# The inverse of the delta rule's triangular matrices: whole 128x128 blocks, or diagonal 64x64 squares in 256 columns

## What is computed

```python
diff = G[..., :, None] - G[..., None, :]
decay = jnp.where(incl, jnp.exp(jnp.where(incl, diff, 0.0)), 0.0)
kk = jnp.einsum("bhnid,bhnjd->bhnij", kc, kc)
lower = jnp.where(strict, bc[..., :, None] * kk * decay, 0.0)
rhs = jnp.concatenate([vc * bc[..., None], kc * (bc * jnp.exp(G))[..., None]], axis=-1)
sol = lax.linalg.triangular_solve(lower + jnp.eye(CHUNK, dtype=f32), rhs, left_side=True,
                                  lower=True, unit_diagonal=True)
```

## Time and profile before

| | |
|---|---|
| median of 3 runs | 2357.48 us (2355.19 to 2358.24) |
| the profiled execution, its own time | 2354.87 us |
| its span | 2352.8 us, 30345 instructions |
| TensorE (PE) | 2188.8 us busy (93%) |
| weight loads (PEld) | 1770.9 us (75%) |
| VectorE (DVE) | 1203.7 us (51%) |
| ScalarE (ACT) | 964.8 us (41%) |
| GpSimd (POOL) | 777.5 us (33%) |
| chain that ended last | PE 74%, DVE 13%, issue 7%, ACT 4% |
| granted TensorE clock | 0.963 of full, mean |

### The profile page before, as it was taken

How to read it: one execution, slowest core, us unless ns; L and a number is a source line. 1 busy time by engine, 2 the same in 40 slices (tenths; PEclk the granted TensorE clock), 3 DMA queues, 4 the chain that set the end, 5 groups by cost and what they waited for, 6 DMA issues and landing times.

```text
span 2352.8 us, 30345 instructions
## 1 busy us (share of the span) xinstructions
PE 2188.8 (93%) x10326; PEld 1770.9 (75%) x10326; DVE 1203.7 (51%) x1824; ACT 964.8 (41%) x1605; POOL 777.5 (33%) x336
## 2 busy tenths in 40 slices
PE   3989898998899999989979999999999989999997
PEld 2768787786678888858847888888866667888886
DVE  6476968754333332269974333323666664333322
ACT  4343453533432332265544444322455554443321
POOL 2631313311344444400004444444311104444442
PEclk8999999999999999989989999999999899999999
DMA  3310201102223233211102233322100002233322
GB/s 120 108 54 28 63 28 46 39 25 77 76 86 94 96 105 99 91 45 54 45 27 84 95 98 98 125 98 82 64 19 18 18 10 90 97 98 98 106 98 72
DMA packets 43638, 169.01 MB, mean 72 GB/s; under 512 B 4848, under 2 KB 4912, under 8 KB 43056
## 3 DMA queue, kind: packets, MB, share of 16 engines
q1 hardware_dynamic: 43056, 163.82, 21.7%
q10 hardware_dynamic: 512, 4.24, 0.5%
HBM read 165.95 MB, written 2.10 MB: 71 GB/s over the span
## 4 chain that ended last, share of the span: by engine, by line
PE 74%; DVE 13%; issue 7%; ACT 4%; POOL 1%; DMA 1%; DVEq 0%; ACTq 0%; POOLq 0%; SPq 0%
PE bank L281 20%; PE bank L282 20%; PE bank L283 20%; PE bank L777 2%; PE bank L764 2%; ACT Pr L1974 1%; POOL WL L246 1%; DVE act_q L954 1%; DVE act_v L954 1%; PE bank L1916 1%; PE bank L1419 1%; PE bank L1418 1%; PE bank L1417 1%; DVE Pr L2092 1%; PE bank L768 1%
## 5 line engine op out<-in xcount | busy, mean ns | idle before, releaser
L246 POOL TENSOR_TENSOR WL<-raw,WR 128x1024 fp32r<-128x1024 f32 (+2 forms) x274 | 712.1, 2599 | 1049.0 <-ACT WR L242 1044.3
L281 PE MATMUL bank<-XR,WR 128*128 128x512 f32 x1528 | 619.6, 405 | 30.1 <-DVE XL L426 15.0
L282 PE MATMUL bank<-XL,WR 128*128 128x512 f32 x1528 | 599.7, 392 | 0.0
L283 PE MATMUL bank<-XR,WL 128*128 128x512 f32 x1528 | 599.2, 392 | 0.0
L242 ACT ACTIVATE WR<-raw 128x1024 fp32r<-128x1024 f32 (+2 forms) x230 | 256.2, 1114 | 758.5 <-PE bank L283 750.7
L281 PEld LDWEIGHTS bank<-XR,WR 128*128 128x128 f32 x1528 | 289.8, 190 | 105.9 <-issue 30.4
L281 PE MATMUL bank<-MR,WR 128*128 128x512 f32 (+1 forms) x856 | 339.3, 396 | 16.2 <-DVE ML L1586 7.6
L282 PEld LDWEIGHTS bank<-XL,WR 128*128 128x128 f32 x1528 | 290.2, 190 | 65.7 <-issue 8.3
L283 PEld LDWEIGHTS bank<-XR,WL 128*128 128x128 f32 x1528 | 289.8, 190 | 61.7
L282 PE MATMUL bank<-ML,WR 128*128 128x512 f32 (+1 forms) x856 | 336.2, 393 | 0.0
L283 PE MATMUL bank<-MR,WL 128*128 128x512 f32 (+1 forms) x856 | 336.0, 392 | 0.0
(11 more groups left out here) (304 smaller groups left out, 2667.5 us busy)
## 6 DMA issues: line engine op xcount, KB each, us to landing
raw<-w SPq DMA_DIRECT2D x224, 512.0 KB, 3.5
raw<-w SPq DMA_DIRECT2D x48, 704.0 KB, 4.0
raw<-w SPq DMA_DIRECT2D x16, 384.0 KB, 3.0
hT<-xT SPq DMA_DIRECT2D x1, 2048.0 KB, 7.5
hT<-xT ACTq DMA_DIRECT2D x1, 2048.0 KB, 7.7
out<-Y SPq DMA_DIRECT2D x8, 256.0 KB, 2.0
memT<-memT ACTq DMA_DIRECT2D x1, 1024.0 KB, 8.1
phi<-phi ACTq DMA_DIRECT2D x1, 1024.0 KB, 6.3
```

The lines of the kernel that those rows point to most:

```text
L246: nc.gpsimd.tensor_tensor(WL[:, here], raw[:, here], WR[:, here].bitcast(F32), ALU.subtract).then_inc(weight_split, 1)
L281: nc.tensor.matmul(into, wr, xr(k0 + k), start=start, stop=False)
L282: nc.tensor.matmul(into, wr, xl(k0 + k), start=False, stop=False)
L283: mm = nc.tensor.matmul(into, wl, xr(k0 + k), start=False, stop=stop)
```

## The change

Until the last level only the two diagonal 64x64 squares of each 128x128 block differ from zero. The change keeps them one above the other: an early square (rows 0 to 63) on partitions 0 to 63, a late one on 64 to 127, four chunks in 256 columns (`NARROW`). T and U of a head now share the tile "T" (`T_`, `U_`); "U" is written only at the end, its lower left part cleared once at the start.

- `square_products`: for each chunk and half one product of 64x64, operands and result on the same half of the partitions, both halves into one bank. `turn_squares`: the early square by a transpose, the late one by a product with the identity.
- kk: three products of 64 columns per chunk (early-early, late-late, late-early), the last kept as the corner.
- The masks are 64 wide; VectorE's and ScalarE's operations in levels 0 to 3 work on 128x256 instead of 128x512; L995 becomes two (early 64x256, late 64x512).
- Level 4's subtraction writes the squares to their places in "U" by two operations per head. Level 5 computes the corner alone: products of 64x64 on one quarter each, and VectorE writes the negative of the result (`tensor_scalar`). The corner is multiplied by beta at level 3's end in place of a mask product.
- The table of constants is 448 columns shorter. `HALF` in a later mixer is renamed `HALVES`.

The core of the diff:

```diff
+        def square_products(into, left, right):
+
+            for b in range(NB):
+                for half in HALVES:
+                    mm = nc.tensor.matmul(into[half, narrow(b)], left[half, narrow(b)], right[half, narrow(b)], start=True, stop=True)
+            return mm
+
+        def turn_squares(e, squares):
+            for b in range(NB):
+                nc.tensor.transpose(bank[6 + e][EARLY, narrow(b)], squares[EARLY, narrow(b)], ident[EARLY, EARLY])
+                mm = nc.tensor.matmul(bank[6 + e][LATE, narrow(b)], squares[LATE, narrow(b)], ident[LATE, LATE], start=True, stop=True)
+            return mm
...
-                    kb = G("keys", e)[:, of_chunk(b)]
-                    mm = nc.tensor.matmul(bank[6 + e][:, of_chunk(b)], kb, kb, start=True, stop=True)
+                    k_early, k_late = (G("keys", e)[:, of_half(b, h)] for h in BOTH)
+                    nc.tensor.matmul(bank[6 + e][EARLY, narrow(b, NARROW)], k_early, k_early, start=True, stop=True)
+                    nc.tensor.matmul(bank[6 + e][LATE, narrow(b, NARROW)], k_late, k_late, start=True, stop=True)
+                    mm = nc.tensor.matmul(bank[6 + e][LATE, narrow(b)], k_late, k_early, start=True, stop=True)
...
+                    if lv < LAST:
+                        square_products(bank[2 + e], joins, U_(e)).then_inc(s_["A_done"], 1)
+                        if lv:
+                            turn_squares(e, U_(e)).then_inc(s_["T_done"], 1)
+                    else:
                         for b in range(NB):
-                            mm = nc.tensor.transpose(bank[6 + e][:, of_chunk(b)], G("U", e)[:, of_chunk(b)], ident)
+                            mm = nc.tensor.matmul(bank[2 + e][EARLY, narrow(b)], G("lower", e)[LATE, narrow(b)], G("U", e)[LATE, of_half(b, 1)], start=True, stop=True)
+                        mm.then_inc(s_["A_done"], 1)
+                        for b in range(NB):
+                            mm = nc.tensor.transpose(bank[6 + e][EARLY, narrow(b)], G("U", e)[EARLY, of_half(b, 0)], ident[EARLY, EARLY])
                         mm.then_inc(s_["T_done"], 1)
...
-                    nc.scalar.activation(As[e], bank[2 + e][:, :], ACT.Identity).then_inc(s_["A_ready"], 1)
+                    nc.scalar.activation(As[e][rows, 0:NARROW], bank[2 + e][rows, 0:NARROW], ACT.Identity).then_inc(s_["A_ready"], 1)
...
-                    V.tensor_copy(G("T", 1), bank[7][:, :]).then_inc(s_["T_moved"][1], 1)
+                    V.tensor_copy(T_(1)[rows], bank[7][rows, 0:NARROW]).then_inc(s_["T_moved"][1], 1)
                 for e in BOTH:
                     dve.wait_ge(s_["U_done"], nth2(e, 6 * p + lv + 1))
-                    V.tensor_tensor(G("U", e), G("U", e), bank[4 + e][:, :], ALU.subtract).then_inc(s_["U_moved"], 1)
...
+                    if lv < LAST - 1:
+                        V.tensor_tensor(U_(e), U_(e), bank[4 + e][:, 0:NARROW], ALU.subtract).then_inc(s_["U_moved"], 1)
+                    elif lv == LAST - 1:
+                        for half in HALVES:
+                            ins = V.tensor_tensor(by_chunk(G("U", e))[half, :, half], by_chunk(U_(e)[half]), by_chunk(bank[4 + e][half, 0:NARROW]), ALU.subtract)
+                        ins.then_inc(s_["U_moved"], 1)
+                    else:
+                        V.tensor_scalar(by_chunk(G("U", e))[EARLY, :, LATE], by_chunk(bank[4 + e][EARLY, 0:NARROW]), -1.0, None, ALU.mult).then_inc(s_["U_moved"], 1)
```

More of the change, by code:

```diff
@@ L100 @@
 N_PARAMS = _at
-IDENT, ONES, TRI, LEVEL0 = 0, 1, 2, 3
-N_CONST = LEVEL0 + LEVELS
+IDENT, ONES, TRI = 0, 1, 2
+N_CONST = 3
+HALF = P // 2
+N_HALF = LEVELS
+HALF_IDENT = LEVELS - 1
 def constant_tables():
@@ L112, in constant_tables @@
     square[:, TRI] = p <= f
-    for s in range(LEVELS):
-        square[:, LEVEL0 + s] = (p >> (s + 1) == f >> (s + 1)) & (p >> s & 1 == 1) & (f >> s & 1 == 0)
+    half = np.zeros((P, N_HALF, HALF), np.float32)
+    r, c = p % HALF, np.arange(HALF)[None, :]
+    for s in range(LEVELS - 1):
+        half[:, s] = (r >> (s + 1) == c >> (s + 1)) & (r >> s & 1 == 1) & (c >> s & 1 == 0)
+    half[:, HALF_IDENT] = r == c
     dist = SEQ - P + p - np.arange(SEQ)[None, :]
@@ L662, in of_chunk, with of_half, narrow, by_chunk @@
             return slice(b * P, (b + 1) * P)
+        LAST = LEVELS - 2
+        HALVES = [slice(0, HALF), slice(HALF, P)]
+        EARLY, LATE = HALVES
+        NARROW = NB * HALF
+        def of_half(b, h):
+            return slice(b * P + h * HALF, b * P + (h + 1) * HALF)
+        def narrow(b, at0=0):
+            return slice(at0 + b * HALF, at0 + (b + 1) * HALF)
+        def by_chunk(tile):
+            return tile.rearrange("p (b n) -> p b n", b=NB)
+        def narrow_of(name, e):
+            return G(name, e)[:, 0:NARROW]
+        def T_(e):
+            return G("T", e)[:, 0:NARROW]
+        def U_(e):
+            return G("T", e)[:, NARROW:2 * NARROW]
         def conv_unit(p, kind, e):
@@ L737, in pair_tensor_g @@
                 pe.wait_ge(s_["T_ready"], nth2(e, c))
-                for b in range(NB):
-                    mm = nc.tensor.transpose(bank[6 + e][:, of_chunk(b)], G("T", e)[:, of_chunk(b)], ident)
-                mm.then_inc(s_["T_turned"], 1)
+                turn_squares(e, T_(e)).then_inc(s_["T_turned"], 1)
             for e in BOTH:
@@ L775, in pair_tensor_g @@
                         pe.wait_ge(s_["k_gained_ready"], nth2(e, c))
-                    for b in range(NB):
-                        mm = nc.tensor.matmul(bank[4 + e][:, of_chunk(b)], G("T", e)[:, of_chunk(b)], As[e][:, of_chunk(b)], start=True, stop=True)
-                    mm.then_inc(s_["U_done"], 1)
+                    if lv < LAST:
+                        square_products(bank[4 + e], T_(e), As[e]).then_inc(s_["U_done"], 1)
+                    else:
+                        for b in range(NB):
+                            mm = nc.tensor.matmul(bank[4 + e][EARLY, narrow(b)], T_(e)[EARLY, narrow(b)], As[e][EARLY, narrow(b)], start=True, stop=True)
+                        mm.then_inc(s_["U_done"], 1)
             gap(2)
@@ L1100, in gdn_vector @@
                 order.link(nc.vector.memset(row[:, 0:8], 0.0))
+            for e in BOTH:
+                order.link(nc.vector.memset(by_chunk(G("U", e))[LATE, :, EARLY], 0.0))
             for kind in range(3):
@@ L1706, in kv_scalar @@
                 for g in range(2):
-                    for rows in (HALF[g], HALF[1 - g]):
-                        nc.scalar.activation(KS[i][g][0][rows, :], k_rows[i][HALF[g], :], ACT.Identity).then_inc(keys_high, 1)
+                    for rows in (HALVES[g], HALVES[1 - g]):
+                        nc.scalar.activation(KS[i][g][0][rows, :], k_rows[i][HALVES[g], :], ACT.Identity).then_inc(keys_high, 1)
             for i in range(2):
@@ L1996, in q_scalar @@
             for g in range(2):
[L1997 removed]
+                nc.scalar.activation(Q_S[j][g][HALVES[g], :], bank[0][HALVES[g], :], ACT.Identity).then_inc(q_high, 1)
         def attend_scalar(act):
```

72 lines of the change are left out of this document (41 added, 31 removed).

## The result

The changed kernel takes 2390.91 us (median of 4 runs, 2385.25 to 2396.64). Runs of the kernel before beside it have a median of 2356.91. The ratio is 1.0146, 95% interval 1.0126 to 1.0166: slower by 34 us, where 2316 was forecast with a range up to 2360. The profiled execution took 2388.0 us, with a span of 2385.9 against 2352.8.

What follows compares the result with a forecast made beforehand. VectorE was taken to bound ahead of the triangular inverse, TensorE within it. 18.7 + 12.2 + 7.0 + 5.4 - 2 = 41.3 us off the profiled 2354.87 gave 2313.6, as median 2316 us; own range 2304 to 2335, overall 2304 to 2360.

Steps and rivals of the forecast that it cites:

- the price of the turn: Inverse's turn, 4 transposes and 4 products (8 passes): 0.47 us side by side against 0.44 before, 0.70 in line.
- a change between whole array and quarters: Some five places per pair where TensorE switches array size, 0.1 us each: 2 us added (0 to 6).
- rival 1: Early and late passes into one bank take turns, in line: net 0, 2357 us, no change; chance 0.18.
- A pass over a quarter: Diagonal quarter passes run side by side in steps of 0.059 us: 0.47 us per product, bounds 0.38 and 0.94.
- Narrow copies: Operations on 128x256: VectorE 0.426 us where 512 columns take 0.69, ScalarE's copy 0.37 where 512 take 0.60.
- Levels 1 to 3: Inverse's levels fall from 4.66 to 3.10 us, set by VectorE's copy and subtraction: 18.7 us won.
- Levels 4 and 5: Inverse's last two levels, level 5 with one corner only, took 9.32 us and win 3.04 per pair: 12.2 us.
- Level 0: Inverse's first level: 2.0 us sooner in pair 0, 1.5 in pair 3, mean 1.75: 7.0 us for four.
- VectorE ahead of the inverse: Shorter VectorE operations before the inverse cut TensorE's pT wait by 1.8 us in pairs 0 to 2: 5.4 us.
- Added: Costs: kk 0.94 us against 0.89, covered in pairs 0 to 2; array switches 2 us; shorter table and clearing 0.
- Rival 2: Clock falls to half in the inverse because quarter passes count for little: 7.4 us lost, 2365 us; chance 0.09.
- being wrong in a way that none of these covers: Closing sign: the gain shows in the levels and comes back as a longer wait for the next pair's rows.

Runs made afterwards that it cites:

- version with products alone: Changed kernel with the early square of a turn also a product with the identity instead of a transposition (level 5's transpositions kept): 2317.42 us, ratio 0.983.
- half by half: Turns by products, plus all four early passes ahead of all four late ones in products and turns: 2326.75 us, ratio 0.9873 against the kernel before.

## Why the prediction was wrong

The step of the prediction that failed is the price of the turn: "The turn is 4 transposes for the early squares and 4 products (8 passes) for the late ones: 0.47 side by side against 0.44 now, 0.70 in line." It priced twelve passes and not their eight goings over. A turn took 1.72 us. With four chunks of 0.43, each three passes in line (0.17) and two goings over, one costs (0.43 - 0.17) / 2 = 0.13.

The size of the miss is read from the version with products alone to the changed kernel: medians 2317.42 and 2390.91, spans of the profiled executions 2317.1 and 2385.9, 68.8 apart. The four inverses are 151.4 - 80.6 = 70.8 us apart, which is all of it. The parts are estimates from the rows above. In the second row 0.34 is what a us at half clock costs, since the same level lasts 5.65 us at full and 8.5 at half clock:

| part | us |
|---|---|
| goings over, at full clock: (5.65 - 3.15) x 16 (levels 1 to 4 of four pairs) | 40 |
| half clock: 89 - 8 us more of it, each at 1 - 5.65 / 8.5 = 0.34 | 27 |
| rest, not assigned | 4 |

The 8.5 us are read between two copies of head 0's join in pair 1:

```profile
301.03 0.38 ACT L970 ACTIVATE SQ<-bank 128x256 f32<-128x256 f32 x1 [4.33 <-PE bank L738]
...
309.58 0.38 ACT L970 ACTIVATE SQ<-bank 128x256 f32<-128x256 f32 x1 [4.76 <-PE bank L738]
```

By the second row the changed kernel would be near 2390.9 - 27 = 2364 us without the fall of the clock, an estimate, and still no win. With the goings over taken away both rows vanish together, as the version with products alone shows. So the goings over cause the whole miss; how they bring the clock down stays open.

Could the trace of before have told? Not this. There a level crosses between products and transpositions four times, and from A0's load at 191.44 to U0's at 194.10 its 24 passes take 2.66 us, 0.111 each, no more than a product's 0.112. On the whole array going over costs nothing, so turn and product seemed to be sums of passes. The prediction did price a change between whole array and quarters (0.1 each, behind L1679 in the earlier trace rows), but counted a transposition of a quarter as one more quarter pass. The page it cited for rival 1 had the missing piece: the Trainium skill, TensorEngine Tiling (Array Packing), states under Key Properties that "Changing tiling mode (not just tile) drains the TensorE", and under Restrictions and Gotchas that tiling by columns excludes transpose mode for f32 input. Taken together, an f32 transposition of 64 columns leaves the mode of the quarter products, and the turn changes modes eight times. The steps agree with that reading, 0.13 us at each quarter transposition's edge and none at a whole one's; no run shows what the array does in them.

By its other steps, in the order of the prediction, measured on the version with products alone:

- **A pass over a quarter.** Right. Early and late passes start 0.022 and 0.036 apart in turn, 0.058 a pair; a product is 0.47 us, as forecast.
- **Narrow copies.** Right: 0.42 and 0.38 against 0.426 and 0.37.
- **Levels 1 to 3.** 3.15 against 3.10: 1.51 x 12 = 18.1 us of 18.7. That VectorE's copy sets the period holds: it stands in the chain of every level, with five of TensorE's six steps. The subtraction of these levels does not stand in it. TensorE's own steps count in full: with less of them side by side (half by half) the level grew to 3.85.
- **Levels 4 and 5.** From A0 of level 4 (193.16, 0.47 behind the start of the 1.15 us row at 192.69) to the projection behind U1 (199.91): 6.75 against 6.28 forecast and 9.32 before, 10.3 us of 12.2. Level 5 keeps four goings over, at 0.13 each; which of them lie on the path, and so make up the 0.47 more, was not separated.
- **Level 0.** What is left of 115.2 - 80.6 = 34.6 is 6.2 us, against 7.0. It is a remainder, not read by itself.
- **VectorE ahead of the inverse.** 5.4 forecast. TensorE's waits for pT and v_beta, 14.3 + 5.9 before, are 13.9 + 0 with products alone, 6.3 us less:

```profile
PE bank L738 <- DVE pT L1087: 13.9, 4, 6.8
```

- **Added.** kk's 48 passes begin at 146.50 and the product behind them at 148.51, 2.01 us for both heads or 1.0 each, change of width included, against 0.94. "The shorter table is loaded behind xT and awaited by nothing early: 0" was off: xT landed after 7.5 us before, and after 7.7 to 8.2 in every kernel with the short table, and the first pair began 2 to 3 us later. Whether the table does that stays open: the kernel with the table padded to its old length gave no time.

The spans differ by 35.7 us: 34.6 in the inverses and 6.1 between them, less 1.2 that the first begins later and 3.8 behind the last one. Of these 3.8 the wait of L1224 for mp has 2.0 (4.0 before, for the same product, and 6.0 now); the prediction had no such term. So the forecast of 2316 fits a kernel that differs from the changed one in one line, 2317.42. Its terms are near, but that closeness is in part luck: the sum was 41.3 and the spans differ by 35.7, while the medians differ by 40.4, because the profiled execution before lies 2.6 us under its median and this one 1.7 over.

**Rivals.** Rival 1 fell: rows of different halves do write one bank at once. The rule cited for it (the Trainium skill, TensorEngine Tiling (Array Packing), Restrictions and Gotchas: different row tiles cannot access the same PSUM bank simultaneously) is not what this trace shows for diagonal quarters, which share no partition: pairs 0.058 us apart, against 0.058 for a single pass in line. Rival 2 saw the half clock, its sign and its place, but gave the wrong reason for it (quarter passes count for little) and so a chance of 0.09 and a price of 7 us; 0.56 was the clock in pair 1's stretch, 0.50 throughout most of levels 1 to 4. Quarter passes alone held 1.00 in the version with products; it took the transpositions among them. The sentence on being wrong in a way that none of these covers looked for a gain that comes back as a wait; what happened in the changed kernel was neither.

## What to carry to other kernels

Count the changes of kind in a stream of small TensorE instructions, not only its passes: on quarters each change between an f32 transposition and a product cost 0.13 us here, more than two passes, and a product with the identity, though twice the passes, was the cheaper turn (0.47 against 1.72 us). A stage that such changes stretch can lose the clock on top. When clock and length are both off, mend the length first and look at the clock again: here it came back with it. A gain that is gone is not a gain that was never there: one line separated 0.983 from 1.0146.

## What the runs showed of the hardware

- Going over between f32 transposition and product: 0.13 us each at 64x64, nothing to be seen at 128x128 (0.111 per pass across four of them).
- Two diagonal quarters run side by side into one bank, 0.058 us per pair of passes; even L818 and L821, which write the same partitions of two banks from different rows, start 0.01 apart.
- The granted clock held at 1.00 over a whole inverse of quarter passes (181.9 to 201.4, busy 18.46 of 19.5 us, products alone). Behind a wait of TensorE (0.15 us busy from 266 to 272) it was at 0.50, and it came back to 1.00 while quarter passes ran.
- With transpositions among the quarter passes it was 0.56 over pair 1's inverse though TensorE read 42.98 busy of 45.2 us; with the same passes waiting for ScalarE, three levels ran at 1.00 with TensorE busy 9.17 of 16 us (194 to 210). The busy share in the records didn't show what the clock followed.
